# Attention schedule: a job's maxima one unit earlier, and its row ahead of the sums' logarithm

## The reference

```
s = einsum('bkgqd,bksd->bkgqs', q_blk, kt) * scale      # full
p = softmax(s, axis=-1);  o = einsum('bkgqs,bksd->bkgqd', p, vt)
s = s + cum_q - cum_k;  s = where(causal, s, -inf)       # forgetting ("fox")
s = where(band, s, -inf); p = softmax(concat([s, sink]))[..., :-1]   # window ("band")
```

## Time and profile before

| what | value |
|---|---|
| median of 3 runs | 2107.11 us |
| the three runs | 2102.16, 2107.14, 2107.11 us |
| time of the profiled execution | 2112.83 us |
| its span, first to last instruction | 2111.0 us |
| mean granted TensorE clock | 0.987 |
| TensorE busy (matmul) | 2027.3 us, 96% |
| VectorE busy | 1102.8 us, 52% |
| ScalarE busy | 878.6 us, 42% |
| full attention, about | 285.4 to 541.6 us of the span |
| band attention, about | 1606.0 to 1746.3 us |
| fox attention, about | 1746.3 to 2003.8 us |

### The profile page before, as it was taken

How to read it: one execution, slowest core, us unless ns; L and a number is a source line. 1 busy time by engine, 2 the same in 40 slices (tenths; PEclk the granted TensorE clock), 3 DMA queues, 4 the chain that set the end, 5 groups by cost and what they waited for, 6 DMA issues and landing times.

```text
span 2111.0 us, 23731 instructions
## 1 busy us (share of the span) xinstructions
PE 2027.3 (96%) x9200; PEld 1580.6 (75%) x9200; DVE 1102.8 (52%) x1531; ACT 878.6 (42%) x1377; POOL 63.3 (3%) x118
## 2 busy tenths in 40 slices
PE   4999999999989999999999999999999999999997
PEld 1778876656778788888888888887787876776575
DVE  5686657656575655534354333346543454345645
ACT  4433345455553432322243222224524663445642
POOL 1001100000000000000000000000010000000000
PEclk9999999999999999999999999999999998999999
DMA  8335410010204556533333333333331010003043
GB/s 340 100 117 201 161 41 11 0 51 1 91 1 150 190 172 193 173 100 122 123 105 133 97 100 101 119 130 124 128 127 51 30 41 22 29 21 130 1 170 120
DMA packets 63198, 217.12 MB, mean 103 GB/s; under 512 B 6640, under 2 KB 7792, under 8 KB 62832
## 3 DMA queue, kind: packets, MB, share of 16 engines
q1 hardware_dynamic: 48944, 161.07, 22.5%
q0 software_dynamic: 14144, 54.53, 7.5%
HBM read 187.79 MB, written 25.17 MB: 101 GB/s over the span
## 4 chain that ended last, share of the span: by engine, by line
PE 87%; DVE 5%; ACT 3%; DMA 2%; issue 2%; SPq 1%; POOL 0%; DVEq 0%; ACTq 0%
PE ps L921 21%; PE ps L922 21%; PE ps L923 21%; PE ps L1054 9%; PE ps L1031 3%; PE ps L1032 2%; PE ps L998 2%; DMA w_raw<-in_weights 1%; PE ps L1013 1%; DMA cmask<-in_consts 1%; SPq L2240 1%; PE ps L1001 1%; PE ps L1142 1%; PE ps L1125 1%; DVE w_lo L1682 1%
## 5 line engine op out<-in xcount | busy, mean ns | idle before, releaser
L921 PE MATMUL ps<-h_hi,w_hi 128*128 128x512 f32 x1488 | 592.7, 398 | 17.0 <-DVE h_lo L1719 10.8
L923 PE MATMUL ps<-h_hi,w_lo 128*128 128x512 f32 x1488 | 582.7, 392 | 0.0
L922 PE MATMUL ps<-h_lo,w_hi 128*128 128x512 f32 x1488 | 582.3, 391 | 0.0
L1682 DVE TENSOR_TENSOR w_lo<-w_raw,w_hi 128x1024 fp32r<-128x1024 f32 x221 | 270.6, 1225 | 488.5 <-ACT w_hi L1278 487.2
L1278 ACT ACTIVATE w_hi<-w_raw 128x1024 fp32r<-128x1024 f32 x222 | 234.7, 1057 | 507.8 <-DMA w_raw<-in_weights 505.9
L921 PEld LDWEIGHTS ps<-h_hi,w_hi 128*128 128x128 f32 x1488 | 281.9, 189 | 80.8 <-issue 12.5
L923 PEld LDWEIGHTS ps<-h_hi,w_lo 128*128 128x128 f32 x1488 | 280.9, 189 | 59.5
L922 PEld LDWEIGHTS ps<-h_lo,w_hi 128*128 128x128 f32 x1488 | 281.4, 189 | 58.0 <-issue 1.9
L1810 DVE TENSOR_REDUCE mh<-ps 128x1 f32<-128x512 f32 x192 | 124.8, 654 | 147.5 <-PE ps L998 69.0
L921 PE MATMUL ps<-hid_hi,w_hi 128*128 128x512 f32 x352 | 136.9, 389 | 0.0
L922 PE MATMUL ps<-hid_lo,w_hi 128*128 128x512 f32 x352 | 136.9, 389 | 0.0
(11 more groups left out here) (311 smaller groups left out, 2644.5 us busy)
## 6 DMA issues: line engine op xcount, KB each, us to landing
w_raw<-in_weights SPq DMA_DIRECT2D x222, 512.0 KB, 3.5
ada_next<-in_ada POOLq DMA_DIRECT2D x32, 512.0 KB, 4.8
ada_last<-in_ada POOLq DMA_DIRECT2D x24, 512.0 KB, 4.3
ada_first<-in_ada SPq DMA_DIRECT2D x8, 1024.0 KB, 14.9
m_scratch<-y POOLq DMA_DIRECT2D x12, 512.0 KB, 5.7
xt<-in_x SPq DMA_DIRECT2D x2, 2048.0 KB, 16.9
y<-m_scratch SPq DMA_DIRECT2D x4, 1024.0 KB, 5.9
x_again<-in_x SPq DMA_DIRECT2D x16, 256.0 KB, 3.7
```

Source lines behind the costliest of these rows:

```text
L921: e.matmul(o, w_hi[slot][:, tile_of(kw)], hi, start=start, stop=False)
L922: e.matmul(o, w_hi[slot][:, tile_of(kw)], lo, start=False, stop=False)
L923: return e.matmul(o, w_lo[slot][:, tile_of(kw)], hi, start=False, stop=stop)
L1682: return e.tensor_tensor(dst, src, hi.bitcast(F32), ALU.subtract)
```

## The change

The last `max` of a job may stand no later than four units ahead of the job's first unit, where it was three. And `mrow` is issued ahead of `take` and `div` of the jobs that have ended. Nothing is added or taken away.

```diff
@@ attention(): places of the maxima
-        high = min(first[i] - 3, end)
+        high = min(first[i] - 4, end)
@@ attention(): the steps of unit g, behind the scores of unit g + 1
-        for step in waiting:
+        rows = [x for x in at_unit.get(g, []) if x[0] == "mrow"]
+        for step in rows + waiting:
             p.add(*step)
         waiting = [("div", *x[1:]) for x in waiting if x[0] == "take"]
-        for step in at_unit.get(g, []) + slots.get(g, []):
+        for step in [x for x in at_unit.get(g, []) if x[0] != "mrow"] + slots.get(g, []):
             p.add(*step)
```

## The result

The changed kernel took 2115.14 us (median of 5 runs, 2113.45 to 2116.14); the kernel before took 2107.11 in the same series (5 runs). The ratio is 1.0042, 95% interval [1.0023, 1.0061]: slower by 0.4%, where 2105.0 and no difference were predicted. Its profiled execution took 2116.14 us, the span is 2114.3 us, and the mean granted clock is 0.990.

A forecast was written before the change was run, and what follows sets the result against it. TensorE, busy 96% of the span, was taken as the bound, so only its gaps and clock could matter. The terms summed to -1.9 us, from the median 2107.1 to 2105.2, say 2105; the 8-in-10 range was 2098 to 2112.

The forecast's parts named there:

- Part 1: Band, 13 even units 2 to 26: the second maximum waits for ScalarE's copy of the row, +6.05 us.
- part 2: Band waits ahead of rows: small ones vanish, -0.45; unit 26's wait shrinks, -1.1, and its lower clock level goes, -1.5.
- part 3: Prologues of full and band: waits for the merge go, smaller waits for the copy come, -0.65 and -1.1 us.
- where the change does nothing: Full and fox outside the listed places: maxima shift but merges and row order stay the same, 0 us.
- Part 4: Unit 28: all four maxima of the first fox job stand there, waits 3.5 for 1.98, +1.5 us.
- part 5: Unit 30: earlier row copy shortens the wait, -1.2 us; the 10.2 us lower-clock stretch goes, -4.4 us.
- Part 6: Unit 31's third maximum waits, +0.8; fox first maxima wait for keys, +3.4, less row waits, -2.6: another +0.8 us.
- part 7: Last row, at 1990.30: one reduction fewer ahead of the merge shortens TensorE's wait for VectorE, -0.65 us.
- the fast rival: Faster by more than 0.3%: band gaps count only as idle time, more lower-clock stretches go; -8.0, or 2099.1; chance 0.16.
- the slow one: Slower by more than 0.3%: the 13 new band gaps pull the clock down; with eight stretches +10, or 2117; chance 0.11.

The follow-up runs named there:

- the second execution: The kernel before, unchanged, profiled and timed once more: median 2105.7 us, span 2101.9 us.
- kernel without the half portion: The change without the additional half portion of fill in its longer prologue: 2115.11 us, ratio 1.0052.
- fox alone: Against the kernel with only the new row order, only the forgetting attention's maxima one unit earlier: 2104.65 us.
- full_only: Against the kernel with only the new row order, only the full attention's maxima one unit earlier: 2099.84 us.
- rows_spread: New row order with maxima in their old places, plus a unit's second and further maxima issued behind its fill: 2097.06 us.
- rows_only: Against the kernel before, only the order changed, `mrow` ahead of `take` and `div`, maxima in their old places: 2096.57 us, ratio 0.996.
- band_only: Against the kernel with only the new row order, only the band jobs' maxima one unit earlier: 2106.29 us.
- change spread: The change with a unit's second and further maxima issued behind its fill portion: 2102.6 us, ratio 0.9992.
- the places alone: Against the kernel before, only the maxima's places changed, `take` still ahead of `mrow`: 2133.1 us, ratio 1.0137.

## Why the prediction was wrong

By medians the change cost 8.0 us beside its own runs of before, and by traces 12.4 (2114.3 against 2101.9); -1.9 was predicted. In short, the largest cost was foreseen, and the gains set against it were not there: 5.9 us of clock that only one execution had paid in full, and 3.6 us in the prologues and in full, where fill had moved. The table sets the prediction's terms against stretches of the two traces (same places of the plan, subtracted; "before" is the second execution). A 0 behind a clock term means that the second execution of before had no such stretch to lose.

| step of the prediction, where | predicted | measured |
|---|---|---|
| 1 and the small waits of 2, band to unit 25 | +5.2 | +6.5 |
| 1 and 2, units 26 and 27; their lower level | -0.7; -1.5 | -1.1; 0 |
| 3, prologues of full and of band | -0.65; -1.1 | +0.8; -0.4 |
| "where the change does nothing": full, up to job (3, 1) | 0 | +1.5 |
| 4, units 28 and 29 | +1.5 | +1.5 |
| 5 and the first of 6, units 30 and 31; the clock | -0.4; -4.4 | +0.7; 0 |
| 6 and 7, fox and its last row | +0.15 | +1.8 |
| stages without an attention, and the rest of full | 0 | +1.0 |

The last row is no effect of the change that can be shown: this execution of the changed kernel has a stretch of 3.4 us at the lower level at 734.2, and no execution of before has it.

**Part 1 held**, mechanism and size: 13 waits for the copy, of 0.30 to 0.62 us, 5.9 in all by starts for 6.05. It is the largest term. The idle column gives seven of them only, 2.0 us, while the stretch of band to unit 23 at an equal clock grew by 6.6 over the order alone. Of that 5.1 are the waits of this kind in it, and they come back when fill hides them; the 1.5 that are left go with the five waits ahead of rows. The Trainium skill (Perfetto Trace Analysis, Identifying the Most-Contended Engine) says that matmul busy time is not a good measure of how close a kernel is to roofline, since matmuls are pipelined. The trace agrees that it misleads: of the 6.6 us, 3.0 stand as busy time (111.49 for 108.47) with no more work done. So the idle column, which the fast rival counted by, leaves out what was really lost. **Part 4 held**: waits of 0.51 and 2.47 by the idle column, and +1.5 in the stretch.

**The step that failed first is the clock's gain in parts 2 and 5**, -1.5 and -4.4. It took two stretches at the lower level from one execution, one that had taken 2112.8 us beside a median of 2107, and booked their going to the waits ahead of them. Two more executions show that the 10.2 us stretch was that execution's own. I had written that the profiled run stood 5.7 us above the median, and then subtracted from the median what explains most of those 5.7 us. The short stretch near unit 26 is there in two of three executions, so some 1.0 of the 1.5 was a fair gain, but not against the execution in the table. Without these 5.9 us the sum is +4.0, or 2111.

**"Where the change does nothing" failed, and with it part 3.** The order of the steps was followed, but not where the fill falls between them. An extra prologue slot brings half a portion: its weight's low part stands on VectorE ahead of the merge (1.23 us at 297.46), so the wait that part 3 saw go stayed, +1.5 against the term. And the phase of the portions shifts for the whole attention: +1.5 in full through two waits beside VectorE's gate work, and, by the kernel with band alone, +2.6 in fox. The kernel without the half portion gives back 1.6 in full, and the 0.9 by which fox in the change exceeds fox alone.

**Part 6 was right in kind and too small.** With fox alone the waits for keys are at the four heads worked out, some 0.3 us longer each (1.04 to 1.21 by starts for 0.67 to 0.96), and the row waits of 0.3 (two), 1.0 and 1.3 do go, as booked at -2.6; three new ones of 0.2 came. These waits make about +2.3; the stretch grew by 1.5, and the difference stays open. The moved portions add the rest: head 3, booked at 0, waits longest, 1.8 by starts. **Of part 7** the wait was 2.29 by the idle column and is 2.13, so 0.16 of the 0.65 is there as a shorter wait. **In part 2** the small waits do go by the order alone (108.93 to 108.47 us in band, -0.46 for -0.45), but the places bring larger ones, since the odd unit lost the `max` that covered them. That TensorE comes earlier where a `max` was taken away was reckoned for unit 26 alone. **In part 5** the row's copy came earlier as worked out (-1.3 with the order alone); the places then took 2.0 back, with third maxima that wait for VectorE.

Of the rivals, the slow one named 2117 and its result is the nearest, but not by its mechanism: band runs at clock 1.00 with its 13 gaps, and the parts add up without a surplus. Behind unit 28 one stretch of 3.4 us stands, at 1754.79, as one did in all three executions of before.

**What would have been faster** is the half of the change whose gains were counted inside parts 2, 4 and 5: the row ahead of `take`, with the maxima left in place. At 2096.57 it beats both kernels. By its trace the gain is -0.5 in band to unit 25, -1.1 in unit 26, -2.7 in unit 28 (1.3 of wait and 1.5 of the lower level that follows it in all three executions of before), -1.3 in unit 30 and -1.1 behind 1981, where the lower level is missing behind the same wait of 2.46 us by starts. That last one is luck of one execution and no gain of the order: full_only and rows_spread, in which that part of fox is as with the order alone, have 3.4 us at the lower level there, from 1974.1 and 1973.8. Unit 28 is another matter, since none of the four kernels with this order and the old places of fox (rows_only, rows_spread, full_only, band_only) has the lower level there. So 5.6 us of the 8 are accounted for, and the rest stays open.

## What to carry to other kernels

A stretch at the lower clock in one profile is not a term of a sum until a second execution has it: when the profiled run is above the median, ask first which rows make it so, and take nothing from them. When steps are moved in a hand-made order, lay the filler work out anew too; half a portion more in a prologue moved waits through the whole of two attentions, with band alone through one whose maxima had not moved. And split a change into its halves before judging it: here one was worth -8 us and the other +19 on top of it.

## What the runs showed of the hardware

- The same kernel's clock differs between executions: 10.2 us at half level in units 30 and 31 in one of three, and 3.4 us near unit 26 in two of three, behind equal waits (2.08 us by starts in two executions, one with and one without such a stretch). Its times spread from 2100.0 to 2112.8 us.
- A stretch of 3.4 us at the lower level cost 1.5 to 1.6 us of time: units 26 to 27 took 1.57 longer in the execution that had one than in the one that had not, with the same waits. The stretch of 10.2 us cost 4.6.
- At unit 28 the lower level followed waits of 1.8 us (before, three executions) and 2.5 (the change and the five other kernels in which four maxima stand together there) by the idle column, and none followed waits of 0.5 and 1.1 (order alone, change spread). At the last row of fox, 3.4 us at the lower level stood in ten of the fourteen executions and not in the other four, with waits of 2.1 to 2.3 in both groups. The 13 waits of 0.3 to 0.6 us in band left it at clock 1.00, and so did those of the kernel with the places alone, some 1.4 us each by the idle column (17.6 in 13).
